# A modulation's weight product taken off TensorE: its sum over feature blocks on VectorE and GpSimd, its loads spread over the dense layers

## The reference

```python
def ada_params(cvec, w, b):
    m = jax.nn.silu(cvec) @ w + b                       # (1, 1024) @ (1024, 9216)
    return m.reshape(cvec.shape[0], N_ADA, 1, D_MODEL)  # nine parts of 1024

def half_ffn(h, shift, scale, gate, g_pre, g_post, w13, w2):
    u = modulate(rmsnorm(h, g_pre), shift, scale)
    return h + 0.5 * gate * rmsnorm(swiglu_2(u, w13, w2), g_post)
```

## Time and profile before

| | |
|---|---|
| median of three runs | 1692.72 us (1686.62 to 1692.78) |
| the profiled execution | 1690.47 us, of which the span of its instructions is 1688.6 us |
| PE busy | 1645.2 us, 97% of the span |
| DVE / ACT / POOL busy | 1037.0 / 837.4 / 152.2 us |
| moved by DMA | 306 MB, 181 GB/s in the mean |
| granted clock of PE | 0.993 of full speed in the mean |

### The profile page before, as it was taken

The page is one execution under the profiler, slowest core; times in us unless marked ns, Lnnn a source line. Parts: engine busy times, 40 slices in busy tenths (PEclk is TensorE's granted clock), DMA queues, the critical chain, the costliest instruction groups (busy, mean ns, idle before and its releaser), DMA issues. The chain is left out here.

```text
span 1688.6 us, 24861 instructions
## 1 busy us (share of the span) xinstructions
PE 1645.2 (97%) x10196; PEld 1419.4 (84%) x10196; DVE 1037.0 (61%) x1339; ACT 837.4 (50%) x1229; POOL 152.2 (9%) x163
## 2 busy tenths in 40 slices
PE   9998999999998999999999999999999999989998
PEld 8995878888776788888888888889889999968886
DVE  5856366664535676657775576658665464676653
ACT  5554435553336365533654465446555344445542
POOL 0232210000001100010001200012000020020000
PEclk9999999999999999999999999999999999999999
DMA  8552297755577777565765676554344142676652
GB/s 258 175 175 101 103 292 206 197 185 195 185 253 248 244 204 198 190 192 152 210 203 175 176 198 184 193 193 150 129 149 151 50 150 90 222 225 185 189 189 86
DMA packets 329160, 306.14 MB, mean 181 GB/s; under 512 B 11953, under 2 KB 286934, under 8 KB 328918
## 3 DMA queue, kind: packets, MB, share of 16 engines
q1 hardware_dynamic: 324390, 296.48, 56.5%
q10 hardware_dynamic: 4384, 7.01, 1.2%
q0 software_dynamic: 272, 1.05, 0.2%
HBM read 303.46 MB, written 1.05 MB: 180 GB/s over the span
## 5 line engine op out<-in xcount | busy, mean ns | idle before, releaser
L406 DVE TENSOR_TENSOR wlo<-raw,whi 128x2048 fp32r<-128x2048 f32 x246 | 565.4, 2300 | 370.8 <-ACT whi L400 370.6
L400 ACT CAST whi<-raw 128x2048 fp32r<-128x2048 f32 x246 | 467.2, 1901 | 253.4 <-PE ps L508 154.1
L450 PE MATMUL ps<-a_split,whi 128*128 128x512 f32 x1760 | 447.5, 394 | 4.0 <-DVE a_split L739 2.7
L450 PEld LDWEIGHTS ps<-a_split,whi 128*128 128x128 f32 x1760 | 316.6, 189 | 64.8 <-issue 8.4
L457 PEld LDWEIGHTS ps<-a_split,wlo 128*128 128x128 f32 x1760 | 240.7, 190 | 18.6 <-DVE wlo L406 0.9
L457 PE MATMUL ps<-a_split,wlo 128*128 128x256 f32 x1760 | 246.3, 282 | 0.4 <-DVE wlo L406 0.4
L442 PE MATMUL ps<-a_split,whi 128*128 128x256 f32 x1280 | 234.8, 286 | 0.0
L442 PEld LDWEIGHTS ps<-a_split,whi 128*128 128x128 f32 x1280 | 201.1, 193 | 0.8
L442 PE MATMUL ps<-a_split,wlo 128*128 128x256 f32 x640 | 181.7, 284 | 0.0
L508 PE MATMUL ps<-whi,fh 128*128 128x512 f32 x440 | 171.5, 390 | 0.0
L508 PE MATMUL ps<-whi,fl 128*128 128x512 f32 x440 | 171.3, 389 | 0.0
(11 more groups left out here) (398 smaller groups left out, 1732.7 us busy)
## 6 DMA issues: line engine op xcount, KB each, us to landing
raw<-in_f_w SPq DMA_DIRECT2D x132, 512.0 KB, 4.6
raw<-in_w_a SPq DMA_DIRECT2D x132, 512.0 KB, 4.4
raw<-in_w_ada SPq DMA_DIRECT2D x72, 512.0 KB, 4.2
raw<-in_w_in SPq DMA_DIRECT2D x68, 512.0 KB, 4.4
raw<-in_w_b SPq DMA_DIRECT2D x66, 512.0 KB, 4.4
raw<-in_a_w_in SPq DMA_DIRECT2D x32, 512.0 KB, 5.3
raw<-in_b_w_qkv SPq DMA_DIRECT2D x24, 512.0 KB, 6.1
raw<-in_a_w_out SPq DMA_DIRECT2D x8, 512.0 KB, 4.6
```

The source lines that it names most:

```text
L400: act.copy(whi[:, c % RING, :], raw[:, r % RING, :]).then_inc(S("hi_ready"), 1)
L406: dve.tensor_tensor(wlo[:, c % RING, :], raw[:, r % RING, :], whi[:, c % RING, :].bitcast(F32), ALU.subtract).then_inc(S("lo_ready"), 1)
L450: return pe.matmul(o[:, :].rearrange("p (s t) -> p s t", s=2), wh[:, k, cols_], a_split[:, :, k, :], start=(k == 0), stop=(k == KD - 1))
```

## The change

The sum over the eight feature blocks of a part leaves PE. DVE and POOL keep a 128x1024 accumulator each, one for the vector `c`, one for `c_ctx`, and add each block times one scalar per partition (`silu_c` is now 8 values per vector). Only the sum over the 128 partitions is left for PE: one product of the accumulators with a table of ones and zeros (`col32`) for each part. [...] The last four parts need one vector only and leave POOL out (`ada_vecs`). A chunk's slot of `raw` is free when both engines are done with it.

More of the change, by code:

```diff
@@ L343, in build, with ada_steps, ada_vecs @@
             last_in[b] = (q, j)
-    ADA_IN_FRONT = {("g_out", 3): range(0, 12), ("up0", 2): range(12, 15), ("m_qkv", 2): [15],
-                    ("m_qkv", 3): [16], ("m_qkv", 5): [17], ("m_qkv", 7): [18], ("m_qkv", 9): [19],
-                    ("m_out", 2): range(20, 28), ("up1", 2): range(28, 31), ("up1", 4): [31],
-                    ("up4", 2): range(32, 36)}
+    ADA_IN_FRONT = {}
[5 more added lines that the diff above has]
+            ADA_IN_FRONT[at_] = [first + i]
+    assert sorted(sum(ADA_IN_FRONT.values(), [])) == list(range(36))
+    def ada_steps(j):
+        return 4 * (j + 1) - (j // 4 + 1)
+    def ada_vecs(part):
+        return (0, 1) if part < 5 else (0,)
     LOADS = []
@@ L1674, in gdn_pe @@
         for s in range(4):
[L1675 removed]
+            unit_pe(pe, 0, s)
             unit_pe(pe, 1, s)
[L1677 removed]
+        unit_pe(pe, 0, 4)
         unit_w_pe(pe, 1, 4)
@@ L2101, in ada_chunk_pe @@
+    def ada_rows_pe(pe, part):
+        pe.wait_ge(*S("ada_used", 8 * part + 8))
+        if part < 5:
+            pe.wait_ge(*S("ada_used1", ada_steps(4 * part + 3)))
+        if part != 3:
+            wait_from(pe, *S("ada", min(part, 3) if part < 5 else part))
+        if part == 4:
+            pe.wait_ge(*evicted("m_qkv", 11))
+        if part == 7:
+            pe.wait_ge(*S("gate_row", 2))
+        vecs = ada_vecs(part)
+        for v in vecs:
             for i in range(4):
-                last = pe.matmul(ada_bank(part)[32 * i:32 * i + 32, 0:256], silu_c(part)[:, 2 * kk + h, :],
-                                 w[:, h, 256 * i:256 * i + 256], start=(kk == 0 and h == 0),
-                                 stop=(kk == 3 and h == 1))
@@ L2118, in ada_take_pe, with silu_c_act @@
         for kind, i in todo:
-            if kind == "chunk":
-                ada_chunk_pe(pe, i)
+            if kind == "rows":
+                ada_rows_pe(pe, i)
             else:
                 ada_cols_pe(pe, i)
-    def silu_c_act(act, n):
+    def silu_c_act(act):
         act.wait_ge(*S("cols_ready", 4))
-        act.wait_ge(*S("silu_zero", n + 1))
-        for w, name in enumerate(("c", "c_ctx")):
-            act.activation(silu_c(3 * n)[:, :, w], col(name, 0, 8), ACT.Silu).then_inc(S("silu_c"), 1)
+        for v, name in enumerate(("c", "c_ctx")):
+            act.activation(silu_c[:, v, :], col(name, 0, 8), ACT.Silu).then_inc(S("silu_c"), 1)
     def ada_row_act(act, part):
-        act.wait_ge(*S("ada_used", 4 * part + 4))
+        act.wait_ge(*S("ada_ps", part + 1))
         wait_from(act, *S("ada_cols", part - 1))
@@ L2143, in mods_dve, with mod_dve @@
     def mods_dve(dve):
-        dve.wait_ge(*S("ada", 8))
-        for i, (w, scale, _, g) in enumerate(MODS):
-            dve.scalar_tensor_tensor(mod_g[:, i, :], ada[:, 8 * scale:8 * scale + 8, w], 1.0,
-                                     col("norm_g", 8 * g, 8), ALU.add, ALU.mult).then_inc(S("mods"), 1)
-        for i in range(3):
-            gate_dve(dve, i)
+        dve.wait_ge(*S("ada", 5))
+        for i in range(4):
+            mod_dve(dve, i)
+        for i in range(2):
+            gate_dve(dve, i)
+    def mod_dve(dve, i):
+        w, scale, _, g = MODS[i]
+        if i == 4:
+            dve.wait_ge(*S("ada", 8))
+        dve.scalar_tensor_tensor(mod_g[:, i, :], ada[:, 8 * scale:8 * scale + 8, w], 1.0,
+                                 col("norm_g", 8 * g, 8), ALU.add, ALU.mult).then_inc(S("mods"), 1)
     def gate_dve(dve, i):
@@ L2193, in gate_rows_pe @@
     def gate_rows_pe(pe, n, h):
+        if h == 0 and n < 2:
+            pe.wait_ge(*S("ada", (7, 9)[n]))
         pe.wait_ge(*S("gate_diag", 2 * n + h + 1))
```

172 lines of the change are left out of this document (65 added, 107 removed).

## The result

The changed kernel takes 1822.5 us (median of 4 runs, 1814.7 to 1825.2) against 1690.9 us before: a ratio of 1.078, 95% interval 1.076 to 1.080. The direction was forecast, the size was not: +132 us instead of +29.

A forecast was written before the change was run, and what follows sets the result against it. PE, busy 97%, was taken to bound the kernel. From 1690.5 us: less 14.2 for removed chunks, plus 7 for new products, plus 36 for stalls (29 first SwiGLU, 2 `m_qkv`, 5 attention) gave 1719 us, range 1688 to 1756.

The forecast's parts named there:

- I take 1.1, near the memset: POOL's multiply of 1024 elements by a scalar: 1.1 us, between 0.95 and 2.4, making a chunk 7.0 us.
- My rival: POOL's multiply costs as much as its add, 2.4 us: a chunk 9.6 us, the total 1755 us; chance 13%.
- the ring: Slot loop: next chunk loads only when POOL is done, lands 4.2 us later, following cuts queue behind; no separate size.
- what must take turns: DVE's and POOL's SBUF work in a pair of up cuts with a chunk: 15.8 us against PE's 11.17.
- the slack of the stage: In the up cuts, DVE's prepared cut may come 7.3 us later before PE waits; subtracted once for the first SwiGLU.
- the attention: POOL's leftover chunks, about 14 us, delay DVE's SBUF operations in each head: +5 us, between 0 and 10.
- Taking turns: A DVE instruction with tensors in SBUF and one on POOL exclude each other, so their times add.
- VectorE's price: DVE's multiply-add of 1024 elements: 1.26 us, so 2.5 us for a chunk.
- The head start at `up0`: PE time saved ahead of `up0`: 1.5 us for chunk 0, 2.5 and 1.9 among 5 to 11, half of 12 to 15.
- `up1` and `up2`: 0, at most 3: Cost in us of the last 16 chunks, where POOL has no part and DVE's work is nearly hidden.
- chunks 32 to 35: Removing them from PE gains 0, as they lie in front of waits of 3.72 and 2.68 us.
- The time without GpSimd's harm: Rival: POOL's instructions fall into DVE's waits, leaving only PE's gain of 7 us: 1683 us; chance 14%.

The follow-up runs named there:

- the cheaper multiply: Changed kernel with GpSimd's scalar multiply written as a product of two tensors, the scalar broadcast, release unchanged: 1791.2 us.
- detached: Changed kernel with GpSimd reading tables instead of the slot, which VectorE alone releases, second vector's product left out: 1743.7 us.
- One number: Changed kernel with SyncE reloading the slot after GpSimd's last multiply of a chunk, not its last add: 1771.1 us, ratio to before 1.047.
- the whole run with 17: Changed kernel with GpSimd holding each slot by 17 one-column multiplies instead of its chunk work, second vector's product left out: 1699.6 us.

## Why the prediction was wrong

**The mis-sized term: GpSimd's multiply, "I take 1.1, near the memset".** It is 2.85 us, outside my bounds of 0.95 to 2.4. I had bounded it from above by the two-tensor add on the belief that one stream in can't cost more than two; it does. A chunk is 10.4 us, not 7.0. At the exchange that the cheaper multiply showed (33 us of work, 31 of time), an estimated 40 x 1.75 = 70 us of the 103 that I missed are this price. My rival had the mechanism but stopped at 2.4 us and at 36 us of effect.

**The missing term: the ring.** "Three slots make it no easier" named it, gave the 4.2 us of landing and the queue behind it, and then left it out of the sum, which went by what must take turns: 15.8 to 17.0 us for a pair. Measured are 21.07 = 15.7 + 5.3. With my 7.0 us, drawn out by turns to some 10, the ring would have been about 15 us (an estimate) and the two accounts would have agreed, so the omission hid; with 10.4 the ring decides. Nor does the ring care for the slack of the stage: in `down0` I had +7 us and it was +29.9, of which the collisions alone make 1.8. For `m_qkv` I had +2 and it was +31.5, for the attention and what follows to `up1` +5 (0 to 10) and it was +12.6. My direction was right for the smaller part of the reason: the collisions that I summed are 47 us, the ring that I left out 79.

**Taking turns: right in kind, too strict.** I held that GpSimd and VectorE exclude each other on SBUF. Between 290.60 and 294.59 the two multiply-adds (2.55 us alone) and GpSimd's scalar multiply (2.85) ran in 4.0 us together, not in 5.4; the operations of two tensors are the ones that shut VectorE out. The scalar multiply itself does wait for VectorE: begun at 297.13, inside L426, it takes 4.76 us, 1.9 more than alone, where L426 had 2.05 left. By my own sum, with 10.4 us for a chunk, a pair has 19.2 us that must take turns, and `up0` would be an estimated 50 us longer with no ring at all; detached it was 20.8. The SBUF page of the Trainium skill ("SBUF — State Buffer", two separate sides) calls the shared ports a lock held for the whole instruction, and a multiply-add with two inputs in SBUF should need it. The trace agrees for GpSimd's operations of two tensors (6.21 us for two multiply-adds) and not for its multiply by a scalar (3.34 us).

**Right.** VectorE's price (1.28 us). The head start at `up0`: 5.7 us, of 7.4 that my fractions for chunks 0 to 14 gave; over all runs it was 3.2 to 7.2, though the programs hardly differ up to there. `up1` free (+0.1 us). The fall of the clock, and that TensorE would wait for `wlo` and `whi`.

**Half right.** "`up1` and `up2`: 0, at most 3" held for VectorE's chunks and not for what I had not costed at all, the turns of rows in their new places: +5.6 us in `up2`. And chunks 32 to 35 were costed at 0 because they lie in waits. Taking them away made nothing earlier, which was right, and lengthened `up4` by 2.3 us through the clock, which I had not costed. The time without GpSimd's harm, which I had put at 1683 us, was 1696, and that with the second vector's product left out. Two slips of the sum changed little: half of the seven chunks around the turns is 3.5 us and not 3.2, and all fractions halved are 7 us and not 10.

## What to carry to other kernels

- Work moved to an engine that shares a ring of load slots adds its time to the slot's hold. Cost the ring first: hold + reload against the period of what else the queue carries. Then look for the release: it belongs behind the last read of the slot, not behind the last step of the job. One number here was worth 51 us of 132.
- A price that no row shows needs an upper bound that doesn't rest on a belief about the operation. Twice the dearest similar row costs nothing to write and would have held this one. Then multiply by the number of uses before you call it a rival.
- Instructions that fill a wait on TensorE are not free to remove: the wait grows and the clock behind it can fall.

## What the runs showed of the hardware

- On GpSimd, 128x1024 float32 in SBUF: a multiply by a scalar takes 2.8 us (per-partition or constant), a product of two tensors with the second broadcast 1.9 us, an add of two full tensors 2.34 us.
- Beside VectorE the cheaper form is the worse neighbour: VectorE's multiply-add took a mean of 1.9 us beside scalar multiplies and adds, 2.8 us where 35 of the 40 multiplies were products of two tensors (1.28 alone). VectorE's instructions on SBUF that begin during GpSimd's operation of two tensors wait for its end, those that begin during a scalar multiply hardly do (2.2 against 0.02 us for the 2048-element subtraction, in the detached run; a multiply-add lost 2.1 against 0.3 there).
- Even one-column operations on GpSimd wait for VectorE: one takes 0.19 us alone, and 2.25 us when it begins 0.1 us into VectorE's 2048-element subtraction (2.28 us). So 17 of them took 2.5 us undisturbed and 5 to 9 us beside VectorE, 40 took 10.3 and 14.85. VectorE isn't held up by them: the whole run with 17 was 3 us above the one without GpSimd's part.
- TensorE's clock, 1.00 at the start of `up4` when idle products filled the waits before it, was 0.76 to 0.88 over the first 12.7 us without them, and `up4` 1.2 to 2.5 us longer than before the change.
